# First tile's opening moves reordered in a two-layer hybrid transformer trunk on one core

## The chip, the core and the metric

The kernel runs on one core of a Trainium2 chip. The core has a matrix engine (TensorE, PE in the rows; PEld is its weight load), a vector engine (VectorE, DVE), a scalar engine (ScalarE, ACT), GpSimd (POOL) and a queue engine that only issues transfers (SyncE, SP). Engines run their own instruction lists in order and wait for one another through semaphores. The metric is the device time of one execution, in microseconds (us), lower being better.

## The reference

Two layers over 256 positions of width 1024. Cut to what matters here:

```
for l in range(DEPTH):                      # DEPTH = 2
    xn = rmsnorm(x, pre_mix_g[l])
    proj = xn @ w_in[l]                     # u, gate, q, k, v, two merge gates
    q, k rotated by cos/sin(positions * inv_freq)
    y_a = rglru_branch(...) @ w_pa[l]
    y_b = sliding_window_attention(...) @ w_pb[l]
    mixed = (gate_a * y_a + gate_b * y_b) @ w_o[l]
    x = x + rmsnorm(mixed, post_mix_g[l])
    x = x + rmsnorm(swiglu(rmsnorm(x, pre_ffn_g[l])), post_ffn_g[l])
```

Everything is float32. The kernel keeps that precision by splitting each operand into a high and a low part and adding three products: high by high, high by low, low by high.

## The kernel before

The 256 positions lie in two tiles of 128 partitions, tile 0 and tile 1. Weights are streamed as panels of 1 MB in a fixed list, `PLAN`: first `kv` 0 and 1 (the rows 0 to 511 and 512 to 1023 of the k and v columns), then `q0` 0 and 1, then `u` 0 to 3, and so on. A panel goes through three stations. SP loads it into one of three raw slots (`weights_raw`; line 486). ACT copies it into the high part (`weights_hi`: `split_hi`, line 1145; `half_hi`, line 1166, for half a panel). DVE subtracts and writes the low part (`weights_lo`: `split_lo`, line 1532; `half_lo`, line 1566). The high and low parts have a ring of four slots. A raw slot is loaded again when DVE has split what was in it; a ring slot is written again when PE has used it.

The activations go a similar way. For each tile ACT squares and sums a row (`mean_square`, line 1150, output `k_tok`), POOL makes the reciprocal root (`rstd_of`, lines 590 and 593), DVE multiplies by it and by the gains (output `q_tok`; lines 1573 and 1581), PE transposes eight blocks into two of the four `work` banks, four in each (lines 745 and 713), ACT copies each bank to `act_a_hi` (`xa_hi`, line 1157) and DVE writes `act_a_lo` (`xa_lo`, line 1558). A matmul of the first panels has a 128x128 block of the activations as its stationary operand and 512 columns of a weight panel as the moving one.

At the start of the program this is done by hand, half a panel at a time, for panels `kv` 0 and 1. SP issues, in this order: x of tile 0, the two halves of `kv` 0, x of tile 1, `kv` 1, six small transfers into `vector_rows`, `q0` 0, the positions, the sinks; then it waits for the split of `kv` 0 to load `q0` 1. ACT's own queue carries the two rows of `pre_mix_g` (line 1130). PE first spreads these gains over the partitions with two matmuls (line 727, into `acc` 2 and 3), then runs five filler transposes of the identity (line 734, `keep_busy(WARM[0])`), turns tile 0 (line 745), runs eight more fillers (`keep_busy(WARM[1])`) and enters `first_products`:

```
for j in range(2):
    pe.wait_ge(*head_split.at(l, j + 1))
    pe.wait_ge(*xa_done.at(l, j + 1))
    t_panel_product("kv", j, acc[:, 0, :], xn_hi, xn_lo, 0, range(0, 2))
    split_ready(AT["kv", j])
    ins = t_panel_product("kv", j, acc[:, 0, :], xn_hi, xn_lo, 0, range(2, 4))
    if j == 0:
        turn_x(l, 0, "xn", 1)
```

`t_panel_product` takes a block's three products one after another (lines 771 to 773), so twelve for each panel and tile. After the 24 products of tile 0 PE does the twelve of `kv` 0 with tile 1, then a transpose of `vector_rows` (line 990), the twelve of `kv` 1 with tile 1, and the panels `q0` 0 and 1 with both tiles.

The order on ACT is: square tile 0, high part of the two halves of `kv` 0, both `xa_hi` of tile 0, square tile 1, high part of the two halves of `kv` 1, both `xa_hi` of tile 1, then whole panels. The order on DVE is: norm of tile 0 in two halves, low part of the first half of `kv` 0, both `xa_lo` of tile 0, low part of its second half, norm of tile 1 in one piece (line 1581), low part of the two halves of `kv` 1, both `xa_lo` of tile 1, the cast of the positions to float (line 1590), then whole panels. POOL, after the two reciprocal roots, waits for that cast and works out the rotary angles in some forty small operations (lines 623 to 641); DVE and ACT make sines from them (lines 1665 and 1204).

Of the kernel before, what the change touches and what calls it, by code (L numbers as in the profile page):

```python
# [25 lines left out]
P = 128  # L26
# [15 lines left out]
WARM = (5, 8)  # L42
# [76 lines left out]
def trunk(nc, x, positions, pre_mix_g, w_in, conv_w, conv_b, lru_wa, lru_ba, lru_wx, lru_bx,  # L119
# [19 lines left out]
    with ExitStack() as ctx:  # L139
# [321 lines left out]
        def _(sp):  # L461
# [35 lines left out]
            first_half(0, 0).then_inc(head_loaded, 16)  # L497
            first_half(0, 1).then_inc(raw_loaded[0].sem, 16)
            sp.dma_start(xres[:, 1, :], x[0, P:S, :]).then_inc(x_loaded[1], 16)
            load(0, 1)  # L500

            for i, part in enumerate((conv_w.rearrange("l c (k p) -> (l c k) p", p=P),
# [5 lines left out]
                if part is None:  # L508

                    for b in range(2):  # L510
# [4 lines left out]
            load(0, 2)  # L515
            sp.dma_start(pos_i[:, :], positions.rearrange("a (t p) -> p (a t)", p=P),
                         allow_slow_non_contiguous=True).then_inc(pos_loaded, 16)
# [184 lines left out]
        def _(pe):  # L702
# [32 lines left out]

            keep_busy(WARM[0])
            for h in range(2):
                dst = claim(0, "xn", h)
                if h == 0:
                    pe.wait_ge(head_normed, 1)  # L740
                else:
                    pe.wait_ge(*xs_done.at(0, 1))
                for k in range(4):
                    f = (4 * h + k) * P
                    ins = nc.tensor.transpose(dst[:, k * P:k * P + P], QTOK[:, 0, f:f + P], ident[:, :])
                ins.then_inc(turned.sem, 1)
            keep_busy(WARM[1])

            def layer(l, first, last_layer):
# [224 lines left out]
                def first_products():  # L974

                    for j in range(2):
                        pe.wait_ge(*head_split.at(l, j + 1))
                        pe.wait_ge(*xa_done.at(l, j + 1))
                        t_panel_product("kv", j, acc[:, 0, :], xn_hi, xn_lo, 0, range(0, 2))
                        split_ready(AT["kv", j])  # L980
                        ins = t_panel_product("kv", j, acc[:, 0, :], xn_hi, xn_lo, 0, range(2, 4))
                        if j == 0:
                            turn_x(l, 0, "xn", 1)
                    ins.then_inc(tile0.sem, 1)
                    pe.wait_ge(*xa_done.at(l, 4))
                    for j in range(2):
# [131 lines left out]
        def _(act):  # L1118
# [9 lines left out]

            for h in range(2):
                act.dma_start(GT[64 * h:64 * h + 1, 0, :], pre_mix_g[0:1, 512 * h:512 * h + 512]).then_inc(gain_row, 16)  # L1130

            def signalled(ins, sem, value):

                ins.then_inc(sem, 1)
# [997 lines left out]
```

## Time and profile before

| what | value |
|---|---|
| time, median of 3 runs | 805.85 us (805.75 to 806.32) |
| the profiled execution's own time | 806.01 us |
| its span, first to last instruction | 804.2 us |
| PE busy in the span | 793.4 us, 99% |
| DVE busy | 601.7 us, 75% |
| ACT busy | 460.2 us, 57% |
| first product of the first panel starts at | 10.69 us |

The profile's own time is 1.8 us more than its span and 0.16 us more than the median. A timeline row gives the start, the length, the engine, the line, what is written and read, and how many instructions the row joins; in brackets stands how long the engine had been idle before it and what ended that. A length with several instructions runs from the first start to the last end. Matmuls overlap, so the pace of a run of them is read from start to start.

### The profile page before, as it was taken

How to read it: one execution, taken by the hardware profiler on the slowest of the kernel's cores; microseconds unless marked ns; L12 is line 12 of the kernel's file. 1: busy time of each engine (PE TensorE's matmuls, PEld its weight loads, DVE VectorE, ACT ScalarE, POOL GpSimd, SP SyncE). 2: the span in 40 equal slices, each digit the busy share in tenths (PEclk: the TensorE clock that was granted, in tenths of full speed). 3: DMA queues.
4: the chain of work that ended last, by engine and by line, in shares of the span. 5: the costliest groups of instructions: out<-in, count | busy, mean ns of one | idle time of the engine just before them, and what ended most of it. 6: DMA issues, size and time to landing. Idle time of an engine off the chain costs nothing.

```text
span 804.2 us, 10534 instructions
## 1 busy us (share of the span) xinstructions
PE 793.4 (99%) x4250; PEld 666.9 (83%) x4250; DVE 601.7 (75%) x602; ACT 460.2 (57%) x591; POOL 76.4 (9%) x135
## 2 busy tenths in 40 slices
PE   7999999999999999999999999999999999999997
PEld 5897898888888888888889889988888888888885
DVE  6799897647689878667489869965567896985762
ACT  5568976643456555535455788865436555465341
POOL 3830000000120000000011200000003100000000
PEclk9999999999999999999999999999999999999999
DMA  9857444445388786862476735434654869768501
GB/s 292 259 208 248 147 139 153 147 168 209 111 307 233 224 309 176 261 213 102 157 225 222 260 129 185 158 108 155 222 196 146 277 184 293 211 223 262 209 0 53
DMA packets 84276, 156.48 MB, mean 195 GB/s; under 512 B 7314, under 2 KB 27906, under 8 KB 84228
## 3 DMA queue, kind: packets, MB, share of 16 engines
q1 hardware_dynamic: 80000, 147.42, 53.6%
q0 software_dynamic: 4224, 8.39, 6.0%
q8 instruction: 34, 0.56, 0.3%
q14 instruction: 14, 0.11, 0.0%
q10 hardware_dynamic: 4, 0.00, 0.0%
HBM read 154.75 MB, written 1.05 MB: 194 GB/s over the span
## 4 chain that ended last, share of the span: by engine, by line
PE 93%; issue 2%; DMA 2%; ACT 1%; DVE 1%; POOL 0%; DVEq 0%; POOLq 0%; ACTq 0%
PE work L771 13%; PE work L773 13%; PE work L772 13%; PE acc L771 9%; PE acc L773 9%; PE acc L772 9%; PE work L763 4%; PE work L764 4%; PE work L765 4%; PE work L857 3%; PE work L858 3%; PE work L859 3%; DMA lru_a<-in_w_ffn_gate 1%; PE work L960 1%; PE acc L885 1%
## 5 line engine op out<-in xcount | busy, mean ns | idle before, releaser
L1532 DVE TENSOR_TENSOR weights_lo<-weights_raw,weights_hi 128x2048 fp32r<-128x2048 f32 x114 | 260.4, 2289 | 88.8 <-ACT weights_hi L1145 88.6
L1145 ACT ACTIVATE weights_hi<-weights_raw 128x2048 fp32r<-128x2048 f32 x116 | 221.6, 1915 | 160.9 <-PE work L773 83.4
L771 PE MATMUL work<-weights_hi,act_a_hi 128*128 128x512 f32 x416 | 164.2, 395 | 0.0
L773 PE MATMUL work<-weights_hi,act_a_lo 128*128 128x512 f32 x416 | 162.4, 390 | 0.0
L772 PE MATMUL work<-weights_lo,act_a_hi 128*128 128x512 f32 x416 | 162.0, 389 | 0.0
L771 PE MATMUL acc<-weights_hi,act_b_hi 128*128 128x512 f32 x240 | 94.8, 395 | 0.0
L773 PE MATMUL acc<-weights_hi,act_b_lo 128*128 128x512 f32 x240 | 93.7, 390 | 0.0
L772 PE MATMUL acc<-weights_lo,act_b_hi 128*128 128x512 f32 x240 | 93.5, 390 | 0.0
L773 PEld LDWEIGHTS work<-weights_hi,act_a_lo 128*128 128x128 f32 x416 | 78.1, 188 | 16.6
L771 PEld LDWEIGHTS work<-weights_hi,act_a_hi 128*128 128x128 f32 x416 | 78.2, 188 | 16.3 <-issue 0.8
L772 PEld LDWEIGHTS work<-weights_lo,act_a_hi 128*128 128x128 f32 x416 | 78.2, 188 | 15.7
L763 PE MATMUL work<-act_a_hi,weights_hi 128*128 128x256 f32 x256 | 73.1, 285 | 0.0
L764 PE MATMUL work<-act_a_lo,weights_hi 128*128 128x256 f32 x256 | 72.5, 283 | 0.0
L765 PE MATMUL work<-act_a_hi,weights_lo 128*128 128x256 f32 x256 | 72.5, 283 | 0.0
L773 PEld LDWEIGHTS acc<-weights_hi,act_b_lo 128*128 128x128 f32 x240 | 45.1, 188 | 9.6
L772 PEld LDWEIGHTS acc<-weights_lo,act_b_hi 128*128 128x128 f32 x240 | 45.1, 188 | 9.1
L771 PEld LDWEIGHTS acc<-weights_hi,act_b_hi 128*128 128x128 f32 x240 | 45.1, 188 | 9.0
L763 PEld LDWEIGHTS work<-act_a_hi,weights_hi 128*128 128x128 f32 x256 | 49.1, 192 | 1.1 <-ACT lru_u L1386 0.8
L764 PEld LDWEIGHTS work<-act_a_lo,weights_hi 128*128 128x128 f32 x256 | 49.2, 192 | 0.1
L765 PEld LDWEIGHTS work<-act_a_hi,weights_lo 128*128 128x128 f32 x256 | 49.2, 192 | 0.0
L590 POOL TENSOR_TENSOR mean_square_eps<-mean_square,eps 128x1 f32<-128x1 f32 x11 | 4.9, 443 | 460.8 <-ACT k_tok L1150 460.8
L1532 DVE TENSOR_TENSOR weights_lo<-q_feat,weights_hi 128x2048 fp32r<-128x2048 f32 x18 | 41.2, 2288 | 5.8 <-ACT weights_hi L1145 5.8
(216 smaller groups left out, 1259.7 us busy)
## 6 DMA issues: line engine op xcount, KB each, us to landing
weights_raw<-in_w_in SPq DMA_DIRECT2D x43, 1024.0 KB, 5.1
weights_raw<-in_w_ffn_gate SPq DMA_DIRECT2D x16, 1024.0 KB, 7.4
weights_raw<-in_w_ffn_up SPq DMA_DIRECT2D x12, 1024.0 KB, 5.7
weights_raw<-in_w_ffn_down SPq DMA_DIRECT2D x12, 1024.0 KB, 4.7
weights_raw<-in_w_pa SPq DMA_DIRECT2D x8, 1024.0 KB, 4.9
weights_raw<-in_w_pb SPq DMA_DIRECT2D x8, 1024.0 KB, 4.9
weights_raw<-in_w_o SPq DMA_DIRECT2D x8, 1024.0 KB, 4.8
q_feat<-in_w_ffn_down SPq DMA_DIRECT2D x6, 1024.0 KB, 8.5
```

What stands on the lines that cost most here:

```text
L763: mm(o, h, hi[:, k, :], start=k == 0, stop=False)
L764: mm(o, h, lo[:, k, :], start=False, stop=False)
L765: last = mm(o, w, hi[:, k, :], start=False, stop=k == KD - 1)
L771: mm(dst, xh, wh, start=first, stop=False)
L772: mm(dst, xh, wl, start=False, stop=False)
L773: return mm(dst, xl, wh, start=False, stop=final)
L857: mm(dst[:, :], xh, wh[:, k, :], start=k == 0 and not adds, stop=False, skip_group_check=adds)
L858: mm(dst[:, :], xh, wl[:, k, :], start=False, stop=False, skip_group_check=adds)
L859: last = mm(dst[:, :], xl, wh[:, k, :], start=False, stop=k == 3, skip_group_check=adds)
L885: last = mm(acc[:, b + par, g * P:g * P + nk], q_rows[rows, c, 2 * g * CHUNK:2 * (g + 1) * CHUNK], KT[rows, g, k0:k0 + nk], start=True, st ...
L1145: activate(w_hi[:, SLOT[n], :], raw_slot(RAWS[n]), ACT.Copy).then_inc(hi_done.sem, 1)
L1532: v.tensor_tensor(w_lo[:, SLOT[n], :], raw_slot(RAWS[n]), bits(w_hi[:, SLOT[n], :]), ALU.subtract).then_inc(split_done.sem, 1)
```

## The change

- SP: x of tile 1 is issued before the second half of `kv` 0; `q0` 0 is issued right behind `kv` 1, ahead of the six transfers into `vector_rows`; the positions leave SP.
- ACT: its queue also carries the positions, behind the two gain rows. The square of tile 1 stands ahead of the first `xa_hi` of tile 0 and of the second half of `kv` 0; the second `xa_hi` stands behind that half.
- DVE: the cast of the positions stands behind the first `half_lo`; the norm of tile 1 is made in two halves (`normed_first`), each with its own signal, and stands ahead of the second `xa_lo` of tile 0.
- PE: the eight fillers behind the turn of tile 0 are gone. Tile 1 is turned by `turn_first`, which starts its first four transposes when the first half is normed. The products of tile 0 are taken two blocks at a time, by kind, each kind with its own wait (`passed`). Tile 1's products of `kv` 0 wait for its first `xa_lo` only, those of `kv` 1 for the second.

On PE, from the fillers to the turn of tile 1, before:

```order
L734 MATMUL work_3<-identity 128x128 x8
L771 MATMUL acc<-weights_hi,act_a_hi 128x512 [waits xa_done,first_half_split]
L772 MATMUL acc<-weights_lo,act_a_hi 128x512
L773 MATMUL acc<-weights_hi,act_a_lo 128x512
L771 MATMUL acc<-weights_hi,act_a_hi 128x512
L772 MATMUL acc<-weights_lo,act_a_hi 128x512
L773 MATMUL acc<-weights_hi,act_a_lo 128x512
L771 MATMUL acc<-weights_hi,act_a_hi 128x512 [waits panel_split_done]
```

and now, from the first product to the turn of tile 1:

```order
L981 MATMUL acc<-weights_hi,act_a_hi 128x512 [waits xa_hi_done,first_half_hi]
L981 MATMUL acc<-weights_hi,act_a_hi 128x512
L981 MATMUL acc<-weights_lo,act_a_hi 128x512 [waits first_half_split]
L981 MATMUL acc<-weights_lo,act_a_hi 128x512
L981 MATMUL acc<-weights_hi,act_a_lo 128x512 [waits xa_done]
L981 MATMUL acc<-weights_hi,act_a_lo 128x512
L981 MATMUL acc<-weights_hi,act_a_hi 128x512 [waits panel_hi_done]
L981 MATMUL acc<-weights_hi,act_a_hi 128x512
L981 MATMUL acc<-weights_hi,act_a_lo 128x512 x2
L981 MATMUL acc<-weights_lo,act_a_hi 128x512 [waits panel_split_done]
L981 MATMUL acc<-weights_lo,act_a_hi 128x512
L744 MATMUL work_2<-identity,q_tok 128x128 [waits first_half_normed]
```

The fillers are gone, and one wait for all operands has become one for each kind of operand.

On DVE, from the low part of the first half of `kv` 0 to the first whole panel (`work_0` to `work_3` are the two halves of tile 0 and of tile 1), before:

```order
L1566 TENSOR_TENSOR weights_lo<-weights_raw,weights_hi 128x1024 [waits first_half_hi]
L1558 TENSOR_TENSOR act_a_lo<-work_0,act_a_hi 128x4x128 [waits xa_hi_done]
L1558 TENSOR_TENSOR act_a_lo<-work_1,act_a_hi 128x4x128 [waits xa_hi_done]
L1566 TENSOR_TENSOR weights_lo<-weights_raw,weights_hi 128x1024 [waits panel_hi_done]
L1581 SCALAR_TENSOR_TENSOR q_tok<-x_residual,rstd,acc 128x1024 [waits rstd_done]
L1566 TENSOR_TENSOR weights_lo<-weights_raw,weights_hi 128x1024 [waits first_half_hi]
L1566 TENSOR_TENSOR weights_lo<-weights_raw,weights_hi 128x1024 [waits panel_hi_done]
L1558 TENSOR_TENSOR act_a_lo<-work_2,act_a_hi 128x4x128 [waits xa_hi_done]
L1558 TENSOR_TENSOR act_a_lo<-work_3,act_a_hi 128x4x128 [waits xa_hi_done]
L1590 CAST pos_float<-pos_int 128x2 [waits pos_loaded]
```

and now:

```order
L1595 TENSOR_TENSOR weights_lo<-weights_raw,weights_hi 128x1024 [waits first_half_hi]
L1611 CAST pos_float<-pos_int 128x2 [waits pos_loaded]
L1587 TENSOR_TENSOR act_a_lo<-work_0,act_a_hi 128x4x128 [waits xa_hi_done]
L1595 TENSOR_TENSOR weights_lo<-weights_raw,weights_hi 128x1024 [waits panel_hi_done]
L1603 SCALAR_TENSOR_TENSOR q_tok<-x_residual,rstd,acc 128x512 [waits rstd_done]
L1603 SCALAR_TENSOR_TENSOR q_tok<-x_residual,rstd,acc 128x512
L1587 TENSOR_TENSOR act_a_lo<-work_1,act_a_hi 128x4x128 [waits xa_hi_done]
L1595 TENSOR_TENSOR weights_lo<-weights_raw,weights_hi 128x1024 [waits first_half_hi]
L1595 TENSOR_TENSOR weights_lo<-weights_raw,weights_hi 128x1024 [waits panel_hi_done]
L1587 TENSOR_TENSOR act_a_lo<-work_2,act_a_hi 128x4x128 [waits xa_hi_done]
L1587 TENSOR_TENSOR act_a_lo<-work_3,act_a_hi 128x4x128 [waits xa_hi_done]
```

The cast and the second `xa_lo` of tile 0 have changed places with what stood between them, and the norm of tile 1 is in two pieces.

On ACT, from the first square to the last `xa_hi`, now:

```order
L1178 ACTIVATE k_tok,mean_square<-x_residual 128x1024 [waits x_loaded_0]
L1194 ACTIVATE weights_hi<-weights_raw 128x1024 [waits first_half_loaded,mean_square_done]
L1178 ACTIVATE k_tok,mean_square<-x_residual 128x1024 [waits x_loaded_1]
L1185 ACTIVATE act_a_hi<-work_0 128x4x128 [waits x_turned,mean_square_done]
L1194 ACTIVATE weights_hi<-weights_raw 128x1024 [waits raw_loaded_0]
L1185 ACTIVATE act_a_hi<-work_1 128x4x128 [waits x_turned]
L1194 ACTIVATE weights_hi<-weights_raw 128x1024 [waits raw_loaded_1]
L1194 ACTIVATE weights_hi<-weights_raw 128x1024
```

The second square has moved up from behind both `xa_hi` of tile 0 to ahead of them and of the second half of `kv` 0.

The heart of the diff, PE's and DVE's side (the moves on SP and ACT are as listed):

```diff
-            keep_busy(WARM[1])
...
+                    pe.wait_ge(head_hi, 1)
+                    pe.wait_ge(*xa_hi_done.at(l, 1))
+                    passed(0, 0, w_hi, xn_hi)
+                    pe.wait_ge(*head_split.at(l, 1))
+                    passed(0, 0, w_lo, xn_hi)
+                    pe.wait_ge(*xa_done.at(l, 1))
+                    passed(0, 0, w_hi, xn_lo)
+                    pe.wait_ge(*hi_done.at(l, 1))
+                    passed(0, 1, w_hi, xn_hi)
+                    passed(0, 1, w_hi, xn_lo)
+                    split_ready(AT["kv", 0])
+                    passed(0, 1, w_lo, xn_hi)
+                    turn_first(1)
+                    pe.wait_ge(head_hi, 2)
+                    pe.wait_ge(*xa_hi_done.at(l, 2))
+                    passed(1, 0, w_hi, xn_hi)
+                    pe.wait_ge(*xa_done.at(l, 2))
+                    passed(1, 0, w_hi, xn_lo)
+                    pe.wait_ge(*head_split.at(l, 2))
+                    passed(1, 0, w_lo, xn_hi)
...
+            def normed_first(t):
+
+                dve.wait_ge(rstd_done.sem, t + 1)
+                for h in range(2):
+                    cols = slice(512 * h, 512 * h + 512)
+                    v.scalar_tensor_tensor(QTOK[:, t, cols], xres[:, t, cols], rstd[:, t:t + 1], acc[:, 2 + h, :],
+                                           ALU.mult, ALU.mult).then_inc(xs_done.sem if h else head_normed, 1)
```

## Rows read from the trace of the kernel before

**Rows 1.** The page: busy time by engine, and shares of the chain that ended last.
```profile
PE 793.4 (99%) x4250; PEld 666.9 (83%) x4250; DVE 601.7 (75%) x602; ACT 460.2 (57%) x591; POOL 76.4 (9%) x135
...
PE 93%; issue 2%; DMA 2%; ACT 1%; DVE 1%; POOL 0%; DVEq 0%; POOLq 0%; ACTq 0%
```

**Rows 2.** PE by windows: stretch, its length, busy, granted clock, DMA, GB/s.
```profile
10.60:14.20 3.60, 3.28 (x16) 1.00 1.06 333
14.20:18.00 3.80, 3.74 (x20) 1.00 1.13 323
18.00:29.20 11.20, 11.20 (x51) 1.00 1.15 289
29.20:60.00 30.80, 30.80 (x249) 1.00 0.61 207
60.00:800.00 740.00, 738.39 (x3900) 1.00 0.58 190
```

**Rows 3.** Timeline of PE, 4 to 18 us.
```profile
4.64 2.08 PE L727 MATMUL acc<-temps,k_feat 1*128 1x512 f32 x4 [4.64 <-DMA temps<-in_pre_mix_g]
...
7.77 1.91 PE L745 MATMUL work<-identity,q_tok 128*128 128x128 f32 x8
9.47 1.46 PE L734 MATMUL work<-identity 128*128 128x128 f32 x8
10.69 0.48 PE L771 MATMUL acc<-weights_hi,act_a_hi 128*128 128x512 f32 x1
...
14.22 1.09 PE L713 MATMUL work<-identity,q_tok 128*128 128x128 f32 x8 [0.34 <-DVE q_tok L1581]
15.35 0.50 PE L771 MATMUL acc<-weights_hi,act_a_hi 128*128 128x512 f32 x1
15.69 0.39 PE L772 MATMUL acc<-weights_lo,act_a_hi 128*128 128x512 f32 x1
...
18.00 0.39 PE L773 MATMUL acc<-weights_hi,act_a_lo 128*128 128x512 f32 x1
```

**Rows 4.** Timeline of SP; then transfers by issue: KB each, us from issue to landing.
```profile
2.15 0.47 SPq L499 DMA_DIRECT2D x_residual<-in_x  x1
2.66 0.45 SPq L486 DMA_DIRECT2D weights_raw<-in_w_in  x1
...
6.23 0.42 SPq L514 DMA_DIRECT2D vector_rows<-in_lru_lambda  x1
...
weights_raw<-in_w_in SPq DMA_DIRECT2D x1, 512.0 KB, 6.4
x_residual<-in_x SPq DMA_DIRECT2D x1, 512.0 KB, 7.2
...
weights_raw<-in_w_in SPq DMA_DIRECT2D x1, 1024.0 KB, 9.6
...
vector_rows<-in_lru_lambda SPq DMA_DIRECT2D x1, 8.0 KB, 7.2
pos_int<-in_positions SPq DMA_DIRECT2D x1, 1.0 KB, 8.6
```

**Rows 5.** Timeline of ACT, 5 to 16 us.
```profile
5.75 1.06 ACT L1166 ACTIVATE weights_hi<-weights_raw 128x1024 fp32r<-128x1024 f32 x1 [0.26 <-DMA weights_raw<-in_w_in]
8.11 1.06 ACT L1166 ACTIVATE weights_hi<-weights_raw 128x1024 fp32r<-128x1024 f32 x1 [1.30 <-DMA weights_raw<-in_w_in]
9.07 1.24 ACT L1157 ACTIVATE act_a_hi<-work 128x512 fp32r<-128x512 f32 x2
10.21 1.05 ACT L1150 ACTIVATE k_tok<-x_residual 128x1024 f32<-128x1024 f32 x1
11.16 0.19 ACT L1150 ACTIVATION_READ_ACCUMULATOR k_tok<-x_residual 128x1 f32 x1
12.32 2.01 ACT L1166 ACTIVATE weights_hi<-weights_raw 128x1024 fp32r<-128x1024 f32 x2 [0.97 <-DMA weights_raw<-in_w_in]
```

**Rows 6.** Timeline of DVE, 6 to 25 us.
```profile
6.75 1.40 DVE L1573 SCALAR_TENSOR_TENSOR q_tok<-x_residual,rstd,acc 128x512 f32<-128x512 f32 x2 [6.75 <-PE acc L727]
...
12.88 1.28 DVE L1581 SCALAR_TENSOR_TENSOR q_tok<-x_residual,rstd,acc 128x1024 f32<-128x1024 f32 x1 [0.71 <-POOL rstd L593]
14.08 2.35 DVE L1566 TENSOR_TENSOR weights_lo<-weights_raw,weights_hi 128x1024 fp32r<-128x1024 f32 x2
16.35 1.28 DVE L1558 TENSOR_TENSOR act_a_lo<-work,act_a_hi 128x512 fp32r<-128x512 f32 x2
...
17.83 2.29 DVE L1532 TENSOR_TENSOR weights_lo<-weights_raw,weights_hi 128x2048 fp32r<-128x2048 f32 x1
...
22.01 2.42 DVE L1532 TENSOR_TENSOR weights_lo<-weights_raw,weights_hi 128x2048 fp32r<-128x2048 f32 x1
```

**Rows 7.** Timeline of POOL, 11 to 25 us.
```profile
17.81 2.93 POOL L623 TENSOR_SCALAR angle<-inv_freq,pos_float 128x32 f32<-128x32 f32 x2 [4.97 <-DVE pos_float L1590]
...
21.94 0.34 POOL L641 TENSOR_TENSOR angle<-angle,turned_by 128x64 f32<-128x64 f32 x1
22.37 2.29 POOL L640 TENSOR_SCALAR turned_by<-turns 128x64 f32<-128x64 f32 x1
```

More of the change, by code:

```diff
@@ L40 @@
 GELU_SCALE = 0.7978845608028654
-WARM = (5, 8)
+WARM = 5
 RAW = 3
@@ L734, in keep_busy, with turn_first @@
                     nc.tensor.transpose(work[3][:, 0:P], ident[:, :], ident[:, :])
[L736 to L746, printed above, removed]
-            keep_busy(WARM[1])
+            def turn_first(t):
+                for h in range(2):
+                    dst = claim(0, "xn", 2 * t + h)
+                    if h == 0:
+                        pe.wait_ge(head_normed, t + 1)
+                    else:
+                        pe.wait_ge(*xs_done.at(0, t + 1))
+                    for k in range(4):
+                        f = (4 * h + k) * P
+                        ins = nc.tensor.transpose(dst[:, k * P:k * P + P], QTOK[:, t, f:f + P], ident[:, :])
+                    ins.then_inc(turned.sem, 1)
+            keep_busy(WARM)
+            turn_first(0)
             def layer(l, first, last_layer):
@@ L984, in first_products, with passed @@
-                    ins.then_inc(tile0.sem, 1)
-                    pe.wait_ge(*xa_done.at(l, 4))
-                    for j in range(2):
+                    def passed(j, half, weights, acts):
+                        wp = t_panel(weights, SLOT[AT["kv", j]], 4)
+                        for k in range(2 * half, 2 * half + 2):
+                            last = mm(acc[:, 0, :], acts[:, 4 * j + k, 0:P], wp[:, k, :],
+                                      start=(j, k) == (0, 0) and weights is w_hi and acts is xn_hi,
+                                      stop=(j, k) == (1, 3) and weights is w_lo)
+                        return last
@@ L987, in first_products @@
+                    passed(1, 1, w_hi, xn_lo)
+                    split_ready(AT["kv", 1])
+                    passed(1, 1, w_lo, xn_hi).then_inc(tile0.sem, 1)
+                    for j in range(2):
+                        pe.wait_ge(*xa_done.at(l, 3 + j))
                         t_panel_product("kv", j, acc[:, 2, :], xn_hi, xn_lo, 1).then_inc(panel_used.sem, 1)
@@ L1130, in _ @@
                 act.dma_start(GT[64 * h:64 * h + 1, 0, :], pre_mix_g[0:1, 512 * h:512 * h + 512]).then_inc(gain_row, 16)
+            act.dma_start(pos_i[:, :], positions.rearrange("a (t p) -> p (a t)", p=P),
+                          allow_slow_non_contiguous=True).then_inc(pos_loaded, 16)
             def signalled(ins, sem, value):
@@ L1151, in mean_square, with xa_hi @@
                                    accum_out=mean_sq[:, n:n + 1]), sem, value)
-            def xa_hi(l, first, name, t):
-                for h in range(2):
+            def xa_hi(l, first, name, t, halves=range(2)):
+                for h in halves:
                     m = first + 2 * t + h + 1
@@ L1171, in _ @@
             half_hi(0, 0).then_inc(head_hi, 1)
+            act.wait_ge(x_loaded[1], 16)
+            mean_square(1, xres[:, 1, :], ms_done.sem, 2)
+            xa_hi(0, 0, "xn", 0, range(1))
             act.wait_ge(*raw_loaded[0].at(0, LOADED[0]))
             half_hi(0, 1).then_inc(hi_done.sem, 1)
-            xa_hi(0, 0, "xn", 0)
-            act.wait_ge(x_loaded[1], 16)
-            mean_square(1, xres[:, 1, :], ms_done.sem, 2)
+            xa_hi(0, 0, "xn", 0, range(1, 2))
             act.wait_ge(*raw_loaded[1].at(0, LOADED[1]))
```

34 lines of the change are left out of this document (11 added, 23 removed).

## The prediction

> **What bounds the kernel now.** I read the page's busy times and chain first: PE is busy in 99% of the span and makes up 93% of the chain [rows 1]. Then PE by stretches: from 18 us on it has no idle time up to 60 us, and 1.6 us in the 740 us behind that [rows 2]. So the kernel is a full matrix engine with a short run-up. Whatever lets PE start its unbroken stretch earlier comes off the end one for one, as long as the weights keep up; nothing else in the opening matters. The reader's mark for it is the first product of tile 1: the last product of tile 0 starts at 18.00 [rows 3], the pace of a product is 0.23 us, so tile 1 starts at **18.22 us**. I ask what this mark becomes.
>
> Before the mark PE has two kinds of loss. It starts its products at 10.69, though fed earlier, behind eight fillers; and it waits for tile 1's turn, which starts at 14.22, released by the norm on DVE [rows 3]. That norm starts at 12.88, released by POOL's root [rows 6]; the root needed ACT's square of tile 1, which ran only at 10.21, behind both `xa_hi` [rows 5]. The products behind the turn start at 15.35 and take 2.87 us to the mark.
>
> **The change, part by part.** I lay the new order out with the old durations.
>
> *Transfers.* x of tile 1 was issued at 2.15 and landed 7.2 us later, at 9.4; the halves of `kv` 0 landed at 5.7 and 8.1, when ACT started on them, and `kv` 1 at about 12.3 [rows 4, 5]. The second half and x have equal size and swap places, so x of tile 1 should land at about 8.1; halfway between its neighbours would be 7.5, so 7.2 at the earliest, and 9.4 as before at the latest. The half of `kv` 0 then lands by 9.4. `kv` 1 keeps its place. The positions go out behind the gains at about 1.5, on another queue; the ACT instruction is about 0.5 us, ahead of a square that waits for x anyway, so free. Before, the positions took 8.6 us to land [rows 4], so 10.1 is the worst case for them; behind their cast on DVE waits the first `xa_lo`, which would then end at 10.8, still ahead of PE's need at 11. The six small transfers lay ahead of `q0` 0 and landed at 13.4 [rows 4]; now a 1 MB panel stands ahead, some 3 us at the 333 GB/s of that stretch [rows 2], so about 16.5. PE asks for them only after the twelve products behind the mark, at about 20: 3 us of cover. `q0` 0 gains.
>
> *ACT.* x at 8.1; the square takes 1.05 and its read 0.19 [rows 5], so the first `xa_hi` starts at 9.3 instead of 9.07 and ends at 9.9. The second half of `kv` 0 follows, 9.9 to 11.0 (before: 8.11 to 9.17). So ACT makes this half 1.8 us **later** than before, the cost of the early square; DVE is late with it too. The halves of `kv` 1 stay bound by their landing: 12.3 to 14.3.
>
> *PE up to the turn of tile 1.* The first product needs only the first `xa_hi`: 9.95 instead of 10.69. Twelve products: two, then two more (the low half was ready before 9.7), two (the first `xa_lo` ends at 10.6), four on the high half ready at 11.0, two on its low part, DVE from 11.0 for 1.2, ready at 12.2. At a pace of 0.23 with the first two or three slower, they end at 13.0.
>
> *DVE is the new bound.* From 11.0 it works without a gap: low part of half a panel 1.13 (two take 2.35), norm in two halves 1.3 to the next instruction (two take 1.40, against 1.28 in one piece), second `xa_lo` 0.6 (two take 1.28), two halves of `kv` 1 2.26, first `xa_lo` of tile 1 0.68 [rows 6]. Running sum: 11.0, 12.1, 13.4, 14.0, 16.3, 17.0. The halves of the norm are there at 12.85 and 13.5, so the turn runs from 13.0 to 14.0, a microsecond ahead of before. The first low half of `kv` 1 is ready at 15.25, the second at 16.4.
>
> *PE to the mark.* High by high and high by low, four products, from 14.05 to 15.1; a wait to 15.3 for the low half; eight more products with a restart of 0.34 (as from 15.35 to 15.69 [rows 3]) give 17.24. The first `xa_lo` of tile 1 is ready at 17.0, just in time. The mark is at **17.24, 1.0 us earlier**. DVE now carries it: where before the norm's late start released PE, the two stalls left are on DVE's low parts.
>
> *POOL beside DVE.* The cast moves from 17.55 to about 9.4, so POOL's angles, before from 17.81 on, now run beside DVE's chain. The rows show what such company costs: POOL's operation at 22.37 took 2.29 us, as long as DVE's 2.42 us one at 22.01 which it had to wait out; and that DVE operation, begun while POOL's 0.34 us one of 21.94 ran, took 0.13 more than its like at 17.83 [rows 6, 7]. The Trainium skill has the rule behind this ("SBUF — State Buffer", section "SBUF: two separate sides"): DVE and GpSimd share one port pair, an exclusive lock, and a DVE operation with two SBUF inputs waits out a GpSimd operation that reads SBUF. The rows agree, and the rule speaks against casting the positions this early. Three low halves of DVE's chain read two SBUF operands. Each can lose from nothing to POOL's 0.34, so 0 to 1.0 us in all; I take two at 0.13, near the one case seen, less what PE's slack hides: **0.1 to 0.3 lost**. The early end of the angles gains nothing, since PE has no idle time around them [rows 2].
>
> *Behind the mark.* The next panel, `q0` 0, is split at about the same time as before (20.1) and needed at about 22.9 instead of 23.9; still covered. Later loads are started by DVE's splits, at most a few tenths later than now, with PE fully busy over them.
>
> **Sum.** 1.0 less for the mark, 0.1 back for POOL: 0.9 us. From the profile's own 806.01 us that is 805.1; the median lies 0.16 below the profile: **805.0 us**. With x landing at 7.2, bound by the turn instead, the mark is some 0.5 earlier: 804.4. No arrangement gives more than about 1.9: `kv` 1 lands at 12.3, and behind it stand one ACT half (1.05), two DVE halves (2.35) and an `xa_lo` (0.68), so 16.4 at the earliest.
>
> **Rivals.**
> *1. The early square stands in the way.* ACT is in order, and `xa_hi`, the second half of `kv` 0, and through it DVE's whole chain are now queued behind the wait for x of tile 1. If x still lands at 9.4, all of DVE's chain is 1.3 later: mark at 18.5, and with POOL's lock at its dear end 18.9. Time 806.1 to 806.5. For it: landing is spread over queues I can't see singly, and 256 scattered elements of positions now go first. Against it: x has moved ahead of 0.5 MB. Chance 0.20.
> *2. Nothing arrives at the end.* The gain is taken back by a later wait, or the reordering only moves idle time within the first 18 us: 805.85, give or take 0.2. Against it: hardly any later idle time to pin it on [rows 2]. Chance 0.12.
> *3. The clock.* The granted clock reads 1.00 throughout [rows 2], but the widths tell that the array ran slower at first: eight transposes took 1.91 us at 7.77 and 1.09 at 14.22 [rows 3], the half-rate level (1.2 GHz) and the full one (2.4). In this profile the full rate was there for the products, behind 6 us of matmuls, spreads and fillers without a pause. Now there is a short pause at about 9.7 and there are the small ones above. The price, by the ratio of the transposes, is about 0.44 us for a product instead of 0.23. Should the full rate come only behind the second turn, the first twelve products last from 9.95 to 15.2, the turn to 16.9, the rest to the mark at 19.9: 1.65 us later than now, **807.5 us, slower**. The point from which it decides: full rate later than about 13 us, where the lost pace outweighs the 1.0 gained. The Trainium skill says of it ("TensorE: Matmul & The Clock Gate", section "Part 1: The HAM clock gate") that the engine rests throttled and activity lifts it, and that how many slow matmuls a kernel sees changes from run to run; by this rule the removed fillers are a risk. The trace bears it out only in that the fast rate came after steady activity. Since products themselves are activity and the pause is some tenths, chance 0.06.
>
> **How the numbers follow.** Forecast 0.62 (804.3 to 805.5), rival 1 0.20, rival 2 0.12, rival 3 0.06. The range that holds 8 in 10 takes the forecast case, rival 2 and the nearer part of rival 1: 804.3 to 806.3. A measurement of this kernel can tell about 0.2%, 1.6 us, from no change. Faster by more needs nearly the whole 1.9 us bound: 0.04. Slower by more is the dear half of rival 3 and a remnant: 0.04. Within: 0.92. A change of sign below that is likely (a small gain), but can't be claimed at 0.2%.
>
> **What would show it.** Right: ACT's second square at about 8.1, first product near 10.0, DVE without a gap from 11 to 18, turn of tile 1 from 13.0, first product of tile 1 near 17.3, PE still full behind it. Rival 1: the second square starts after 9. Rival 3: products of the first panel 0.4 apart. POOL's lock: low halves of 1.3 us or more. Wrong altogether: a wait of PE beyond 18 us that isn't there now, above all for `vector_rows` or `q0` 0.

## The result: slower, and outside the range

| | before | changed |
|---|---|---|
| median, 13 runs each, taken side by side | 806.1 us (805.66 to 807.02) | 807.76 us (806.39 to 808.37) |
| the profiled execution's own time | 806.01 us | 807.91 us |
| its span | 804.2 us | 806.1 us |

The ratio is 1.0017, 95% interval 1.001 to 1.0025. Forecast was 805.0 us with 804.3 to 806.3; the changed kernel is 1.7 us slower instead of 0.8 faster. Rival 3 gave nearly this time (807.5), but by luck: in the profile 0.86 of the 1.9 us are lost in the opening, where it said, and the rest far behind it.

The page of the changed kernel, the lines that answer to [rows 1], and the same windows of PE as [rows 2]:

```profile
PE 794.1 (99%) x4242; PEld 667.0 (83%) x4242; DVE 601.4 (75%) x603; ACT 460.1 (57%) x591; POOL 73.4 (9%) x135
...
PE 88%; DMA 3%; DVE 3%; ACT 2%; issue 2%; POOL 0%; SPq 0%; DVEq 0%; POOLq 0%; ACTq 0%
```

```profile
10.60:14.20 3.60, 3.60 (x9) 1.00 1.05 389
14.20:18.00 3.80, 3.80 (x21) 1.00 1.07 320
18.00:29.20 11.20, 11.20 (x51) 1.00 1.18 286
...
60.00:800.00 740.00, 739.03 (x3911) 1.00 0.60 190
```

Two things are to be seen. In the first window PE is busy all the time and yet has only 9 matmuls in it, where it had 16 (twelve products and the last fillers). And in the chain PE's share has fallen from 93 to 88%, with DMA and DVE up: something in the body now breaks PE's chain.

**The opening.** Timeline of PE in the changed kernel, the counterpart of [rows 3] (a row of two or more joins that many products):

```profile
7.35 1.92 PE L744 MATMUL work<-identity,q_tok 128*128 128x128 f32 x8
10.47 1.19 PE L981 MATMUL acc<-weights_hi,act_a_hi 128*128 128x512 f32 x2 [1.20 <-ACT act_a_hi L1185]
11.46 1.05 PE L981 MATMUL acc<-weights_lo,act_a_hi 128*128 128x512 f32 x2
12.31 1.05 PE L981 MATMUL acc<-weights_hi,act_a_lo 128*128 128x512 f32 x2
...
14.87 0.74 PE L981 MATMUL acc<-weights_lo,act_a_hi 128*128 128x512 f32 x2
15.45 1.03 PE L744 MATMUL work<-identity,q_tok 128*128 128x128 f32 x8
16.24 0.70 PE L981 MATMUL acc<-weights_hi,act_a_hi 128*128 128x512 f32 x2
...
19.08 0.39 PE L772 MATMUL acc<-weights_hi,act_a_hi 128*128 128x512 f32 x1
```

From 11.46 to 12.31 two products take 0.85: 0.43 each, the level of 1.2 GHz, where the later ones take 0.23. The full rate is there at about 15.1; before, it was there for the first product. So the twelve products last 5 us, the turn of tile 1 starts at 15.45 instead of 14.22, and the mark is at **19.08, 0.86 later** than before. The granted clock still reads 1.00 here; the pace tells the level, that column doesn't.

ACT and DVE, the counterparts of [rows 5] and [rows 6]:

```profile
8.55 1.06 ACT L1178 ACTIVATE k_tok<-x_residual 128x1024 f32<-128x1024 f32 x1 [1.84 <-DMA x_residual<-in_x]
9.51 0.19 ACT L1178 ACTIVATION_READ_ACCUMULATOR k_tok<-x_residual 128x1 f32 x1
9.73 0.60 ACT L1185 ACTIVATE act_a_hi<-work 128x512 fp32r<-128x512 f32 x1
```

```profile
11.30 1.23 DVE L1595 TENSOR_TENSOR weights_lo<-weights_raw,weights_hi 128x1024 fp32r<-128x1024 f32 x1 [0.25 <-ACT weights_hi L1194]
12.45 1.40 DVE L1603 SCALAR_TENSOR_TENSOR q_tok<-x_residual,rstd,acc 128x512 f32<-128x512 f32 x2
13.77 0.68 DVE L1587 TENSOR_TENSOR act_a_lo<-work,act_a_hi 128x512 fp32r<-128x512 f32 x1
14.37 2.48 DVE L1595 TENSOR_TENSOR weights_lo<-weights_raw,weights_hi 128x1024 fp32r<-128x1024 f32 x2
16.77 1.28 DVE L1587 TENSOR_TENSOR act_a_lo<-work,act_a_hi 128x512 fp32r<-128x512 f32 x2
```

DVE's chain is the forecast one, 0.3 late: it runs without a gap from 11.3 to 18.0. It is not what PE waits for. The halves of the norm are ready by 13.8, and PE, at half rate, takes them at 15.45.

**The body.** I followed DVE's `weights_lo` of the load `q_feat` and its `v_tok` behind it in both profiles. In layer 0 they start at 261.26 and 267.88 before, 262.14 and 269.42 now: **0.88** and **1.54** late. In layer 1, 654.96 and 662.10 before, 656.34 and 663.99 now: **1.38** and **1.89** late. So 0.9 us come from the opening and two steps of about 0.5 from two places in the FFN, one in each layer (between them 0.16 is won back: 1.54, then 1.38). The chain of the changed kernel shows the first (start, length, what); before, this stretch of the chain is nothing but PE:

```profile
254.96 10.22 DMA lru_a<-in_w_ffn_gate
...
265.26 1.93 ACT weights_hi L1173
...
269.42 0.69 DVE v_tok L1949
...
270.16 0.50 PE work L858
```

A panel lands late, ACT makes its high part, DVE its low part, and behind that on DVE stands the `v_tok` addition that frees a bank for PE. The panel's transfer, before and then in the changed kernel (last number: us from issue to landing):

```profile
lru_a<-in_w_ffn_gate SPq DMA_DIRECT2D x1, 1024.0 KB, 9.4
```

```profile
lru_a<-in_w_ffn_gate SPq DMA_DIRECT2D x1, 1024.0 KB, 10.2
```

The same panel takes 0.8 longer, among the same two neighbours. What differs is a fourth party. DMA queues in 254.6 to 263, most of the time in which the three panels load, before and then changed (packets, MB, share of 16 engines; `q1` has less in the changed kernel because the loads are issued 0.88 us later and the stretch is the same):

```profile
q0 software_dynamic: 516, 1.02, 69.7%
q1 hardware_dynamic: 566, 1.13, 37.1%
```

```profile
q0 software_dynamic: 527, 1.05, 72.9%
q1 hardware_dynamic: 344, 0.70, 24.1%
q8 instruction: 1, 0.02, 0.7%
```

`q8` brings instructions. The whole run has 34 such packets (0.56 MB, so 16 KB each), and the 8,500 matmuls and weight loads of PE over 34 are 250 to a packet. Before, one falls at 253.5 us, just ahead of the three panels' data, which flow from 254.3 on; now it falls at 258.7, among them. It is 16 KB, and its share, 0.7% of 16 engines over 8.4 us, is 0.94 us of one engine's time. If a panel is spread over all engines, it lands when its last part does, and a delay of one engine delays the panel; this is argued from the sizes, since the profile doesn't tell the 16 engines apart.

In layer 1 the packet moved from 651.5 to 655.8. But there it lay among the panels before, too: the same panel, issued and landing as follows, was on its way from 647.8 to 657.9.

```profile
647.77 0.37 SPq L486 DMA_DIRECT2D lru_a<-in_w_ffn_gate  x1
...
lru_a<-in_w_ffn_gate SPq DMA_DIRECT2D x1, 1024.0 KB, 10.1
```

So "ahead" against "among" is a difference of layer 0 alone. The change took eight fillers away, which are 16 instructions, a weight load and a matmul each (x4250 to x4242 for PE and PEld), and that shifts the rest of PE's list against the borders of the packets. The Trainium skill has the form of this ("Runtime: NRT & Kernel Launch", section "Instruction fetch mechanics"): an engine's instruction memory is refilled in blocks of 16 KB, 256 instructions, by DMA while it runs. The rows agree in the size of a packet, and nearly in the count. It calls the cost of crossing such a border mostly hidden. For PE itself the trace agrees: in the changed kernel it has no idle time from the packet's start at 258.7 until 269.9. For a panel that loads beside the packet, the runs below show a cost.

### The profile page after: what moved, and what is told of

The parts are those of the page before. It is cut to its first block, busy times and chain, and to the rows that moved or that the text cites. A ratio compares the mean times of both kernels' runs of the same rounds, so it can differ in the third digit from the quotient of the medians.

```text
span 806.1 us, 10519 instructions
## 1 busy us (share of the span) xinstructions
PE 794.1 (99%) x4242; PEld 667.0 (83%) x4242; DVE 601.4 (75%) x603; ACT 460.1 (57%) x591; POOL 73.4 (9%) x135
## 4 chain that ended last, share of the span: by engine, by line
PE 88%; DMA 3%; DVE 3%; ACT 2%; issue 2%; POOL 0%; SPq 0%; DVEq 0%; POOLq 0%; ACTq 0%
PE work L772 12%; PE work L774 12%; PE work L773 12%; PE acc L772 8%; PE acc L774 8%; PE acc L773 8%; PE work L764 4%; PE work L765 4%; PE work L766 4%; PE work L858 3%; PE work L859 3%; PE work L860 3%; DMA lru_a<-in_w_ffn_gate 3%; ACT weights_hi L1173 1%; DVE weights_lo L1561 1%
```

## The experiments

Each has 11 executions, beside 33 of the kernel before with medians of 806.11 (e1 to e4), 806.16 (e5 to e8) and 806.19 us (e9 to e12). "Late" columns give how much later than before something starts in the profile: the mark, `v_tok` of layer 0, `v_tok` of layer 1. An "idle wait" is a wait of PE that is satisfied when it comes; two make one instruction. "Landing" is that of `lru_a` in layer 0.

| kernel | instructions of PE against before | packet of layer 0 at | landing | mark late | layer 0 late | layer 1 late | median, us |
|---|---|---|---|---|---|---|---|
| changed | -16 | 258.7 | 10.2 | 0.86 | 1.54 | 1.89 | 807.76 |
| e1: fillers back | 0 | 252.6 | 9.7 | -0.61 | -0.34 | -0.13 | 805.67 |
| e2: before, no fillers | -16 | 258.0 | 10.5 | -0.49 | 0.93 | 1.88 | 807.75 |
| e3: square behind | -16 | 257.3 | 10.5 | -0.79 | 0.22 | 0.58 | 806.63 |
| e4: e3, 3 fillers | -10 | 257.2 | 10.4 | -0.74 | 0.22 | 0.37 | 806.79 |
| e5: 32 idle waits | 0 | 253.5 | 9.7 | 0.30 | 0.47 | 0.33 | 806.40 |
| e6: e3, 8 fillers ahead | 0 | 252.4 | 9.6 | -0.77 | -0.61 | -0.42 | 805.75 |
| e7: e2, 32 idle waits | 0 | 253.2 | 9.7 | 0.03 | 0.17 | 0.04 | 806.50 |
| e8: e3, 32 idle waits | 0 | 252.7 | 9.7 | -0.58 | -0.34 | -0.26 | 805.78 |
| e9: waits between layers | -16, then 0 | 258.7 | 10.7 | 0.33 | 1.52 | 1.57 | 807.25 |
| e10: before, 32 idle waits | +16 | 252.3 | 9.4 | -0.01 | 0.02 | 0.32 | 805.79 |
| e11: e3, 64 idle waits | +16 | 251.4 | 9.7 | -0.43 | -0.30 | 0.00 | 805.73 |
| e12: e8, late cast | 0 | 252.9 | 9.6 | -0.76 | 0.04 | 0.15 | 806.21 |

**e1: the fillers back in the changed kernel.**

```diff
             turn_first(0)
+            keep_busy(8)
```

> The changed kernel with its eight fillers behind the turn of tile 0 put back, nothing else. Clock theory (without fillers PE pauses 1.2 us, from 9.3 to 10.5, and the full rate comes only at 15.1, so the first twelve products go 0.43 us apart): with fillers the rate is full by about 11, the products go 0.23 apart, DVE's chain sets the mark (first product of tile 1) at about 17.6 instead of 19.08; time about 1.5 us below the changed kernel, near 806.3 or less. Order theory (the loss lies in the new order on ACT and DVE, and in the later wait near 664 us, and the clock is beside the point): the mark stays at 18.5 or later and the time within 0.4 us of the changed kernel, 807.4 to 808.1.

Median 805.67 (805.46 to 806.31), ratio 0.9994, 0.9985 to 1.0003. PE in it:

```profile
9.49 1.70 PE L732 MATMUL work<-identity 128*128 128x128 f32 x8
10.95 0.70 PE L982 MATMUL acc<-weights_hi,act_a_hi 128*128 128x512 f32 x2
11.48 0.63 PE L982 MATMUL acc<-weights_lo,act_a_hi 128*128 128x512 f32 x2
```

With no pause the full rate is there by the second pair, and the mark is 0.61 earlier than before. One line takes the whole loss away; but it restores both the activity and the length of PE's list, so it can't tell the two causes apart.

**e2: only the fillers out of the kernel before.**

```diff
-            keep_busy(WARM[1])
```

> The kernel before without its eight second fillers, nothing else. Clock theory: PE then pauses from 9.5 to about 10.4 and the full rate comes several us later than 10.6; the first twelve products take about 5.2 us instead of 2.9, the mark moves from 18.2 to about 20, time 807.5 to 808.5 against 806.1. Order theory: the first product starts up to 0.3 us earlier, tile 1's turn is still released by DVE at 14.2, time unchanged, 805.8 to 806.3.

Median 807.75 (806.65 to 808.48), ratio 1.0018, 1.0009 to 1.0027: the whole loss of the changed kernel from this one line. But the opening isn't the slow one that I expected:

```profile
4.07 2.08 PE L727 MATMUL acc<-temps,k_feat 1*128 1x512 f32 x4 [4.07 <-DMA temps<-in_pre_mix_g]
...
7.20 1.94 PE L745 MATMUL work<-identity,q_tok 128*128 128x128 f32 x8
10.10 0.47 PE L770 MATMUL acc<-weights_hi,act_a_hi 128*128 128x512 f32 x1 [0.96 <-DVE act_a_lo L1557]
10.41 0.39 PE L771 MATMUL acc<-weights_lo,act_a_hi 128*128 128x512 f32 x1
10.64 0.39 PE L772 MATMUL acc<-weights_hi,act_a_lo 128*128 128x512 f32 x1
```

A pause of a microsecond, and still 0.23 from product to product. The mark is 0.49 earlier than before, because the gains landed earlier in this execution (4.07 against 4.64), and layer 1 is 1.88 late. So the loss lies behind the mark, and the clock alone can't be the story. Of these 2.4 us, 0.9 and 0.4 go at the two places; the other 1.1 seep away in small pieces, half of it by 261 us (`weights_lo` of `q_feat` is 0.05 late) and half between the two places, and no run shows why. This profile reads a granted clock of 0.95 for the whole span, the other ten executions 0.998 or 0.999. That e2 and the changed kernel have the same median is therefore in part chance: their losses are made up differently.

**e3: the second square behind the first `xa_hi`, still no fillers.** On ACT, in the changed kernel (`mean_square` is the square):

```diff
+            xa_hi(0, 0, "xn", 0, range(1))
...
-            xa_hi(0, 0, "xn", 0, range(1))
```

The line goes from behind the square of tile 1 to ahead of it.

> The changed kernel with one exchange on ACT: the first xa_hi of tile 0 stands ahead of the square of tile 1 again; still no second fillers. The first xa_hi then starts with the turn at about 8.6 instead of 9.73, and PE's pause shrinks from 1.2 us to 0.3 or less. If it is the pause that kept the clock down: full rate by about 11, mark at 17.4 to 17.8, time 805.5 to 806.3. If it is the mere lack of fillers, whatever the pause: full rate near 15 again; products start a microsecond earlier but 0.43 apart, mark at 18.0 to 18.7, time 806.8 to 807.6. Order theory: the square is 0.6 later, DVE's chain too, time as the changed kernel or up to 0.6 worse.

Median 806.63 (806.33 to 807.22), ratio 1.0007, 0.9998 to 1.0016. The opening did what was expected: first product at 9.13, full rate from 10.97, mark at 17.43.

```profile
9.13 1.19 PE L981 MATMUL acc<-weights_hi,act_a_hi 128*128 128x512 f32 x2
10.12 1.01 PE L981 MATMUL acc<-weights_lo,act_a_hi 128*128 128x512 f32 x2
10.97 0.63 PE L981 MATMUL acc<-weights_hi,act_a_lo 128*128 128x512 f32 x2
```

The time did not: 0.79 gained at the mark, 1.0 lost again by `v_tok` of layer 0 and 0.36 more in layer 1.

**e4: e3 with three fillers behind the turn of tile 0.**

```diff
             turn_first(0)
+            keep_busy(3)
```

> As the one before, with three fillers behind the turn of tile 0, so that PE has no pause at all. Clock theory: full rate by about 11, mark at 17.4 to 17.8, time 805.3 to 806.0, at or below the kernel before. Order theory: 807.4 or more.

Median 806.79 (806.37 to 807.57, and one execution of 1612.89 that nothing here explains). Like e3: a shorter list by 10 instructions has its packet at 257.2 and loses as much.

**e5: 32 idle waits at the start of PE's list in the changed kernel.** No work is added, the list has its old length.

```diff
+            for _ in range(32):
+                pe.wait_ge(ones_done, 1)
             pe.wait_ge(ones_done, 1)
```

> The changed kernel with 32 waits on a semaphore that is long set, at the very start of PE's program, where PE sits idle for the gains until about 4 us: 16 instructions more for PE, no work and no time, so PE's program has the length that it had before (8714 instructions instead of 8698). Fetch theory (PE's instructions arrive in packets of 16 KB on a DMA queue of their own; without the 16 filler instructions the packet near 253 us comes at 258 us, inside the three large transfers of the feed-forward stage, and delays their landing, once in each layer): the packet is back near 254, the wait of PE at 269 us is gone or under 0.1 us and the one near 663 is 0.3 to 0.6 instead of 0.8, time 0.6 to 1.0 us below the changed kernel, 806.8 to 807.2; the clock stays late, first product of tile 1 at about 19. Chance theory (the landings there vary by themselves): 807.5 to 808.1, waits as in the changed kernel. Clock theory alone: no change either.

Median 806.40 (805.72 to 807.32), 1.36 below the changed kernel, more than I expected, since in its profile the opening was better too (full rate at 13.8, mark at 18.52). From 261 us to the end nothing more is lost: 0.35 late at `weights_lo`, 0.33 in layer 1. So the 1.36 are the packet's and the better opening's together.

**e6: e3 with eight fillers at the very start of PE's list**, ahead of its wait for the gains, a place where PE idles anyway.

```diff
+            pe.wait_ge(ident_done, 1)
+            for _ in range(8):
+                nc.tensor.transpose(work[3][:, 0:P], ident[:, :], ident[:, :])
...
-            pe.wait_ge(ident_done, 1)
```

> The changed kernel with its first xa_hi ahead of the square of tile 1, and with eight fillers at the very start of PE's program, ahead of its wait for the gains, where PE is idle. They cost nothing, make PE's program as long as before (8714), and may bring the full rate earlier. Both theories together: first product at about 9, full rate by 10.9 or sooner, first product of tile 1 at 17.2 to 17.6, no wait at 269 us; time 804.8 to 805.4, 0.7 to 1.3 below the kernel before. Chance theory: as the same kernel without early fillers, 806.3 to 806.9.

Median 805.75 (805.08 to 806.25), ratio 0.9995, 0.9986 to 1.0003. Half as expected: the packet is out of the way and the gain survives, but the early fillers didn't bring the full rate sooner (about 11.6, against 10.95 in e3).

**e7: e2 with 32 idle waits**, the lines of e5 and the one of e2, which puts the fetch theory to the kernel before.

> The kernel before without its eight second fillers and with the 32 idle waits at the start, so that only the fillers' activity is missing and PE's program is as long as before. It splits the 1.65 us that their removal cost (807.75 against 806.1). Fetch theory: 0.9 us or more of it come back, 806.3 to 806.9, no wait at 269 us. Chance theory or clock theory alone: 807.5 to 808.

Median 806.50 (806.04 to 807.37), as expected, 1.25 below e2; 0.04 late in layer 1. Here too PE paused (0.97) and had no slow product.

**e8: e3 with 32 idle waits**, the lines of e5 put into e3.

> The changed kernel with its first xa_hi ahead of the square of tile 1 and with the 32 idle waits; no fillers at all beyond the five. The same kernel without the waits took 806.63, with its first product of tile 1 at 17.4, 0.85 earlier than before, and lost it at 268 us. Fetch theory: no wait at 268 us, packet near 253, time 805.1 to 805.7. Chance theory: 806.3 to 806.9.

Median 805.78 (805.43 to 806.14), ratio 0.9994, 0.9986 to 1.0003: 0.85 below e3, a little above the expected range. Of the 0.58 gained at the mark 0.26 is left.

**e9: the 32 idle waits between the two layers.** The changed kernel's opening and first layer stay as they are; the second layer has the old positions.

```diff
                         down_panel(j, 1, False, j == end).then_inc(panel_used.sem, 1)
+                    for _ in range(32):
+                        pe.wait_ge(ones_done, 1)
```

> The changed kernel with 32 satisfied waits on PE (16 instructions) put between the two layers instead of at the start. The opening and the whole first layer have the changed kernel's instruction positions, the second layer has the old ones. Theory of instruction fetch (where a 16 KB packet of PE's program falls among the FFN loads decides the later loss): the wait of PE near 269 us stays at 0.4, the one near 663 falls from 0.8 to 0.3 to 0.5, the packet near 655.8 goes back to about 652 to 653; time 807.2 to 807.5, half of what the waits at the start gave back, with some 0 to 0.5 us for the waits themselves taken off that gain. Rival theory (the 32 waits helped only because they stand at the start of PE's list and shift its opening and clock): no change against the changed kernel, 807.7 to 807.9.

Median 807.25 (806.0 to 808.1), in the expected range. Its executions scatter, five of the eleven at 806.0 to 806.7, and the profile is of one at 807.6; e5's is of one at its median. With that said, this is the clearest pair, for its profile and that of e5 come out of the opening alike: `weights_lo` at 261.60 and 261.61. DVE in e5, then in e9:

```profile
261.61 2.29 DVE L1563 TENSOR_TENSOR weights_lo<-q_feat,weights_hi 128x2048 fp32r<-128x2048 f32 x1 [0.21 <-ACT weights_hi L1175]
...
266.14 2.29 DVE L1563 TENSOR_TENSOR weights_lo<-lru_a,weights_hi 128x2048 fp32r<-128x2048 f32 x1
268.35 0.68 DVE L1951 TENSOR_TENSOR v_tok<-work,v_tok 128x512 f32<-128x512 f32 x1
```

```profile
261.60 2.29 DVE L1563 TENSOR_TENSOR weights_lo<-q_feat,weights_hi 128x2048 fp32r<-128x2048 f32 x1 [0.21 <-ACT weights_hi L1175]
...
267.19 2.29 DVE L1563 TENSOR_TENSOR weights_lo<-lru_a,weights_hi 128x2048 fp32r<-128x2048 f32 x1 [1.09 <-ACT weights_hi L1175]
269.40 0.68 DVE L1951 TENSOR_TENSOR v_tok<-work,v_tok 128x512 f32<-128x512 f32 x1
```

ACT's work on `lru_a` in the two, and its landing in e9:

```profile
264.18 1.92 ACT L1175 ACTIVATE weights_hi<-lru_a 128x2048 fp32r<-128x2048 f32 x1 [2.12 <-DMA lru_a<-in_w_ffn_gate]
```

```profile
265.24 1.92 ACT L1175 ACTIVATE weights_hi<-lru_a 128x2048 fp32r<-128x2048 f32 x1 [3.18 <-DMA lru_a<-in_w_ffn_gate]
```

```profile
lru_a<-in_w_ffn_gate SPq DMA_DIRECT2D x1, 1024.0 KB, 10.7
```

Nothing in the programs but the place of 16 empty instructions differs up to here, and ACT starts on the panel 1.06 later. In layer 1, where e9's list has its old positions (packet at 652.9), it loses 0.05 more by `v_tok` (1.52 to 1.57), where the changed kernel lost 0.35 (1.54 to 1.89). That alone shows nothing of layer 1: e10 and e11, with the packet at 651.6, lose 0.30 there.

**e10: 32 idle waits in the kernel before**, with the fillers: the lines of e5 and nothing else: a test whether idle waits help by themselves.

> The kernel before with 32 satisfied waits on PE at the start, nothing else: 16 instructions more than before, fillers and orders as they were. Instruction fetch: the packet near 253.5 us comes no later than before (252 to 253.5) and stays clear of the three FFN loads; no wait near 269; time 805.9 to 806.4, as before. If idle waits at the start help by themselves, whatever the fetch does, it should be 0.5 to 1.3 us faster than before: 804.8 to 805.6.

Median 805.79 (805.58 to 806.46), ratio 0.9997, 0.9988 to 1.0006: no difference that shows, though 0.1 under the expected range. The packet comes at 252.3, ahead of the panels, and layer 0 is 0.02 late. By the medians the waits themselves bring 0.4 us at most, which isn't shown to differ from nothing and is less than the 0.85 to 1.36 of e5, e7 and e8.

**e11: e3 with 64 idle waits**, the loop of e8 over 64.

> The variant with the second square behind the first xa_hi, now with 64 idle waits on PE at its start instead of 32 (32 instructions). Instruction fetch: the packet near 252.6 comes up to 1.5 us sooner and is as clear of the loads as before, so 805.6 to 805.9, like the variant with 32 (805.78). If more waits as such are better: below 805.3. If the waits begin to delay PE's opening (the mark later than 17.7): above 806.0.

Median 805.73 (805.3 to 806.03), ratio 0.9993, 0.9984 to 1.0002, as expected. Being further ahead of the panels is worth no more than being ahead of them.

**e12: e8 with the cast of the positions at its old place on DVE**, behind both `xa_lo` of tile 1.

```diff
             half_lo(0, 0).then_inc(head_split.sem, 1)
-            dve.wait_ge(pos_loaded, 16)
-            v.tensor_copy(pos_f[:, :], pos_i[:, :]).then_inc(pos_done, 1)
...
             xa_lo(0, 0, "xn", 1)
+            dve.wait_ge(pos_loaded, 16)
+            v.tensor_copy(pos_f[:, :], pos_i[:, :]).then_inc(pos_done, 1)
             split_lo(0, 2)
```

> The variant with the second square behind the first xa_hi and 32 idle waits, with the cast of the positions back at its old place on DVE, behind both xa_lo of tile 1, so that POOL's angles no longer run beside DVE's chain. The prediction's term for the shared port says 0.1 to 0.3 lost with the early cast: low halves of kv 1 back from 2.48 to 2.35 us for the two, the mark at most 0.2 earlier, time 805.5 to 805.8 against 805.78. If the angles have no cover at their old place once the mark is earlier, PE waits behind 20 us and the time is over 806.0.

Median 806.21 (805.72 to 806.64), 0.43 above e8, the second of the two outcomes. The two halves of `kv` 1 take 2.35 us on DVE instead of 2.39 in e8, so the shared port costs 0.04 there. But most of the mark's 0.76 is gone by 53 us, where 0.15 is left. DVE and PE:

```profile
41.51 0.20 DVE L1698 TENSOR_SCALAR angle<-angle 128x64 f32<-128x64 f32 x1 [1.94 <-POOL angle L639]
...
51.91 1.09 PE L926 MATMUL work<-lru_uc,q_feat 64*64 64x256 f32 x16 [0.52 <-DVE lru_uc L1718]
```

DVE waits 1.94 us for POOL's last angle (1.53 already in the kernel before, at 41.35), and PE is no longer behind it but ahead. In e8 the angles are done at 32.9 and DVE doesn't wait. The early cast is what lets an earlier mark through.

**What the landings say together.** Where the packet falls among the panels of layer 0 (changed, e2, e3, e4, e9) `lru_a` takes 10.2 to 10.7 us; where it falls ahead of them (before and the eight others) it takes 9.4 to 9.7. No kernel lies between. In layer 1 those with 16 or 10 instructions less up to there (changed, e2, e3, e4) have 10.4 to 10.6 and the others 10.1 to 10.6. They overlap, and the packet, at 651.1 to 655.8, lies among the panels in every kernel, the one before included; that fits with none of them having the 9.4 to 9.7 of layer 0, but what makes the difference within layer 1 stays open. An earlier PE seems to meet it more (e1, e6 and e11, all early, have 10.4 to 10.6), yet e8, as early, has 10.3. So the packet's part is shown for the first of the two steps; for the second it is not. Left open too is why the packet of layer 0 moved by 4 to 5 us, where 16 instructions of a pace of 0.23 us for two are 1.8 us of work. The packets aren't evenly spaced in PE's list: from one to the next it starts 197 to 305 matmuls and weight loads before, 197 to 307 in the changed kernel.

## Why the prediction was wrong, step by step

*Transfers: right, a little optimistic.* x of tile 1 landed at 8.55 (forecast 8.1), the second half of `kv` 0 by 10.2, `kv` 1 at 12.6, the positions in time. Rival 1's condition (the second square after 9) didn't come.

*ACT and DVE: right.* The chain on DVE was laid out to a tenth in its lengths, 0.3 late in its start, and it would nearly have carried the forecast of 17.24 for the mark: it is at 17.61 in e1, which has the changed kernel's order, and at 17.64 and 17.43 in e8 and e3.

*POOL's port: right in kind, small.* 2.48 against 2.35 for two halves in the changed kernel, 2.39 in e8: 0.04 to 0.13, about the 0.1 that the sum took.

*PE up to the turn: the first step that failed.* "At a pace of 0.23 with the first two or three slower, they end at 13.0." They ended at 15.4, ten or eleven of them slow. The pause that I called "short" and "some tenths" was 1.20 us, since the first `xa_hi` stood behind the square, which stood behind x; 0.4 of it came because the gains landed earlier (4.23 against 4.64) and PE was done with tile 0's turn sooner. The price that rival 3 set for a product (0.44) is what was measured (0.43), and so is its condition (full rate later than about 13); the price was luck in part, as the ratio of the transposes that it named, 1.91 to 1.09, gives 0.40. I gave it 0.06 because products are activity themselves. Its size was 0.86 and not 1.65 in this profile: it counted the second turn and what follows as slow too, while its first twelve products were right (15.2, measured 15.4). The rival's rule from the Trainium skill, that the number of slow matmuls changes from run to run, is borne out: e9 has the opening of the changed kernel, instruction for instruction, and reached the full rate at 14.0 instead of 15.1, with the mark at 18.55. And e2 and e7 paused for 0.96 and 0.97 and never slowed.

*"Behind the mark": the second step that failed, and nobody's rival.* I had taken it that later loads move by tenths with PE full over them, and costed the fillers' removal by their time alone. [rows 2] hold 1.6 us of idle PE in 740, 0.3 of it at 662 by the pace of products, where DVE had just waited 0.43 for the high part of `lru_a`: a place without any cover, there to be seen before. The removal also shifts PE's instruction list by 16, and a 16 KB packet of it now falls into the three panels of layer 0. By the medians the old length gives back 1.36 (changed to e5), 1.25 (e2 to e7) and 0.85 us (e3 to e8). The first of these is too much for the packet, since the mark of e5's profile is also 0.56 earlier; in the second the mark is 0.52 later and e2's small losses are gone too. What the opening is worth can be estimated from two pairs that differ by the place of the square alone: 1.13 us of median for 1.65 at the mark (e3 to changed) and 0.62 for 0.88 (e8 to e5), 0.7 to one. By this 0.4 of the 1.36 and about 0.6 of the whole loss of 1.66 are the slow opening's, and about 1.0 is the list's. The marks are of single profiles, so this division is rough.

*"The early end of the angles gains nothing": right for the kernel before, wrong for the changed one.* PE had no idle time around them because it came no earlier than they did. e12 shows 0.4 to 0.7 us that the early cast is worth once the mark moves.

*"One for one": overstated.* Even with the packet out of the way in layer 0, of 0.43 to 0.77 us gained at the mark 0 to 0.42 is left in layer 1 (e11 0, e1 0.13, e8 0.26, e6 0.42), since the landing there doesn't come forward with PE. The best variants, e1, e6, e8 and e11, lie at 805.67 to 805.78, 0.4 us under the kernel before that was measured beside them; all four intervals include 1, so none is shown to be faster. And e10, which gains nothing at the mark, lies at 805.79 as well, so the 0.4 can't be put down to the new order.

## What to carry to other kernels

Filler work on a matrix engine does two jobs, it keeps the pace up and it sets where the rest of its instruction list lies; a prediction of its removal must price both, and an experiment that puts fillers back must be paired with one that puts back only the length. Look in the page for the queue that carries instructions, and in the body for the one transfer whose landing has no slack: that is where a change in the first 20 us can come back 250 us later. And a row that shows no wait shows only that the other engine was on time for the present schedule; ask of each such neighbour how much earlier it could be.

## What the runs showed of the hardware

PE's instructions come in 34 packets of 16 KB (queue `q8`), each about 1 us of one DMA engine's time. With one packet among three 1 MB panels of layer 0 a panel landed 0.5 to 1.3 us later (10.2 to 10.7 against 9.4 to 9.7, 14 kernels), and as that panel had no slack there, the kernel lost up to 1.0 us (e9: DVE's `weights_lo` of `q_feat` is 0.34 late in layer 0 and, at 656.33, 1.37 late in layer 1). Sixteen empty instructions at the start of the list undid it. The rate of PE after a pause was not the same for like openings: full rate at 13.8, 14.0 and 15.1 us in e5, e9 and the changed kernel (pauses of 1.17, 0.71 and 1.20), at 10.97, 11.8 and 9.8 in e3, e8 and e12, whose PE has the same opening with hardly a pause, and no slow product at all in e2 and e7 behind pauses of 0.96 and 0.97. The granted clock of the profile didn't follow: it read 1.00 where products took 0.43, and 0.95 for all of e2, whose products took 0.23.
